# Moving four small subtractions to GpSimd and one weight sum behind another, in a two-model transformer kernel on one core

## The reference, cut to what matters

```python
def swiglu(h, w_in, w_out):                  # w_in: 1024 x 5632, w_out: 2816 x 1024
    gate, up = jnp.split(h @ w_in, 2, axis=-1)
    return (jax.nn.silu(gate) * up) @ w_out
...
x = x + FFN_HALF * swiglu(rmsnorm(x, ffn1_norm[l]), ffn1_w_in[l], ffn1_w_out[l])
x = x + hybrid_mixer(...)
x = x + FFN_HALF * swiglu(rmsnorm(x, ffn2_norm[l]), ffn2_w_in[l], ffn2_w_out[l])
```

## Time and profile before

| | |
|---|---|
| three runs | 2625.32, 2626.52, 2627.41 us; median 2626.52 |
| profiled execution | 2627.41 us, its span 2625.3 us |
| TensorE busy | 2608.7 us (99%), 15755 matmuls; granted clock 0.999 |
| VectorE busy | 2031.5 us (77%) |
| ScalarE busy | 1546.2 us (59%) |
| GpSimd busy | 116.0 us (4%) |
| DMA | 474.18 MB, mean 181 GB/s |

### The profile page before, as it was taken

One profiled execution on the slowest core, in us unless ns is written; L12 is line 12 of the kernel. 1 busy time (PEld: TensorE's weight loads), 2 busy tenths in 40 slices (PEclk: granted clock), 3 DMA queues, 4 the chain that ended last, 5 costly groups with the idle time before them and its releaser, 6 DMA issues.

```text
span 2625.3 us, 38060 instructions
## 1 busy us (share of the span) xinstructions
PE 2608.7 (99%) x15755; PEld 2293.6 (87%) x15755; DVE 2031.5 (77%) x2073; ACT 1546.2 (59%) x1703; POOL 116.0 (4%) x146
## 2 busy tenths in 40 slices
PE   9999999999999999999999999999999999999998
PEld 7889999988888899999888889999888889999887
DVE  8887854698798686547988995676997995676987
ACT  6656674465565567644656555555756555655655
POOL 0000170000000003400000000000000000000000
PEclk9999999999999999999999999999999999999999
DMA  6746545466475554545747465444755646543663
GB/s 218 241 157 200 158 145 175 136 224 227 152 239 170 170 166 160 176 130 179 245 161 232 163 206 176 153 145 153 240 193 189 204 163 193 158 137 129 225 232 104
DMA packets 388778, 474.18 MB, mean 181 GB/s; under 512 B 28855, under 2 KB 348671, under 8 KB 388352
## 3 DMA queue, kind: packets, MB, share of 16 engines
q1 hardware_dynamic: 384190, 469.86, 55.2%
q10 hardware_dynamic: 4418, 1.90, 0.3%
HBM read 466.09 MB, written 5.64 MB: 180 GB/s over the span
## 4 chain that ended last, share of the span: by engine, by line
PE 90%; DVE 5%; ACT 2%; issue 1%; DVEq 1%; DMA 0%; ACTq 0%
PE bank L421 27%; PE bank L423 27%; PE bank L422 27%; PE bank L988 1%; DVE w_lo L408 1%; PE bank L572 1%; DVE conv_acc L2165 1%; PE bank L1828 1%; PE bank L1804 1%; DVE w_lo L1216 0%; ACT w_hi L402 0%; DMA raw<-in_ffn_w_down 0%; DVEq L2977 0%; DVE part L2975 0%; DVE neg_max L2676 0%
## 5 line engine op out<-in xcount | busy, mean ns | idle before, releaser
L421 PE MATMUL bank<-w_hi,xn_hi 128*128 128x512 f32 (+2 forms) x1568 | 581.9, 371 | 1.7 <-DVE xn_lo L552 1.4
L423 PE MATMUL bank<-w_hi,xn_lo 128*128 128x512 f32 (+2 forms) x1568 | 573.1, 366 | 0.0
L422 PE MATMUL bank<-w_lo,xn_hi 128*128 128x512 f32 (+2 forms) x1568 | 572.5, 365 | 0.0
L408 DVE TENSOR_TENSOR w_lo<-raw,w_hi 128x2048 fp32r<-128x2048 f32 (+2 forms) x190 | 412.1, 2171 | 197.6 <-ACT w_hi L402 197.2
L1108 ACT ACTIVATE w_hi<-raw 128x2048 fp32r<-128x2048 f32 x192 | 367.4, 1913 | 138.2 <-DMA raw<-in_ffn_w_down 42.8
L1216 DVE TENSOR_TENSOR w_lo<-raw,w_hi 128x2048 fp32r<-128x2048 f32 x192 | 438.1, 2282 | 1.2 <-ACT w_hi L1108 1.2
L402 ACT ACTIVATE w_hi<-raw 128x2048 fp32r<-128x2048 f32 (+3 forms) x199 | 359.7, 1808 | 76.5 <-PE bank L423 74.1
L421 PE MATMUL bank<-xn_hi,w_hi 128*128 128x256 f32 (+1 forms) x1376 | 397.0, 289 | 1.0 <-DVE w_lo L408 1.0
L422 PE MATMUL bank<-xn_lo,w_hi 128*128 128x256 f32 (+1 forms) x1376 | 389.1, 283 | 0.0
L423 PE MATMUL bank<-xn_hi,w_lo 128*128 128x256 f32 (+1 forms) x1376 | 389.1, 283 | 0.0
L421 PEld LDWEIGHTS bank<-w_hi,xn_hi 128*128 128x128 f32 x1568 | 296.2, 189 | 49.7 <-DVE xn_lo L552 2.3
(11 more groups left out here) (394 smaller groups left out, 4149.7 us busy)
## 6 DMA issues: line engine op xcount, KB each, us to landing
raw<-in_w_in SPq DMA_DIRECT2D x122, 1024.0 KB, 5.3
raw<-in_ffn_w_in SPq DMA_DIRECT2D x126, 512.0 KB, 5.2
raw<-in_ffn_w_out SPq DMA_DIRECT2D x44, 1024.0 KB, 5.0
raw<-in_ffn_w_down SPq DMA_DIRECT2D x44, 1024.0 KB, 5.2
raw<-in_ffn_w_gate SPq DMA_DIRECT2D x64, 512.0 KB, 4.8
raw<-in_ffn_w_up SPq DMA_DIRECT2D x64, 512.0 KB, 6.0
block<-in_ffn_w_in SPq DMA_DIRECT2D x48, 512.0 KB, 7.1
block<-in_ffn_w_gate SPq DMA_DIRECT2D x24, 512.0 KB, 6.8
```

Source lines behind the costliest of these rows:

```text
L408: dve.tensor_tensor(in_order(kind, slot, w_lo), as_loaded(kind, slot), in_order(kind, slot, w_hi).bitcast(F32), ALU.subtract).then_inc(s_l ...
L421: pe.matmul(out, a_hi, b_hi, start=start, stop=False, skip_group_check=check)
L422: pe.matmul(out, a_hi, b_lo, start=False, stop=False, skip_group_check=check)
L423: return pe.matmul(out, a_lo, b_hi, start=False, stop=stop, skip_group_check=check)
```

## The change

1. The four `mixed_lo` subtractions of each FFN move from VectorE to GpSimd (`ffn_pool`), in the order 0, 1, 3, 2; TensorE's waits count in that order.
2. ScalarE converts the mixed tiles in other places of `first_ones`, with only number 0 ahead of the hidden values of unit 0, and both gates of unit 1 stand ahead of hi("dn", 1).
3. In the first pair of units of each FFN, VectorE runs lo("t2"), `hide`, lo("b22"), `sum_t4`, lo("t3"). The other two pairs keep the old order.
4. GpSimd's wait for the constants moves from the start of its program into `mixer1_pool`.

```diff
+        MIXED_LO = (0, 1, 3, 2)
...
+        def mixed_lo_count(f, i):
+            return 4 * f + MIXED_LO.index(i) + 1
...
             def x_mixed(i):
-                pe.wait_ge(s_xsumlo, mixed_count(f, i))
+                pe.wait_ge(s_xsumlo, mixed_lo_count(f, i))
...
             def first_ones():                      # ScalarE
                 hi("dn", 0)
-                for i in MIXED:
-                    mixed_hi(i)
+                mixed_hi(0)
                 hi_hidden(0)
+                mixed_hi(2)
                 hi("b11", 2)
-                first_gate(1)
+                gates(1)
                 hi("dn", 1)
-                second_gate(1)
+                mixed_hi(1)
                 hi_hidden(1)
+                mixed_hi(3)
                 hi("b21", 2)
                 hi("t1", 2)
...
                 lo("dn", 0)                        # VectorE, first_ones
-                mixed_lo(0)
                 lo_hidden(0)
                 sum_t1(2)
                 lo("b11", 2)
                 hide_from_bank(1, 0)
-                mixed_lo(2)
                 hide_from_bank(1, 1)
                 lo("dn", 1)
                 lo_hidden(1)
                 sum_t2(2)
                 lo("b21", 2)
                 lo("t1", 2)
-                mixed_lo(1)
                 sum_t3(2)
...
             def two(u):                            # VectorE
                 lo("t2", u)
-                sum_t4(u)
-                hide(u, 0, bank[4][:, 256:512], gate_act[:, 0, :])
                 if u == TWOS[0]:
-                    mixed_lo(3)
-                lo("b22", u)
+                    hide(u, 0, bank[4][:, 256:512], gate_act[:, 0, :])
+                    lo("b22", u)
+                    sum_t4(u)
+                else:
+                    sum_t4(u)
+                    hide(u, 0, bank[4][:, 256:512], gate_act[:, 0, :])
+                    lo("b22", u)
                 lo("t3", u)
...
+        def ffn_pool(pool, p, f):
+            def mixed_lo(i):
+                pool.wait_ge(s_xsumhi, mixed_count(f, i))
+                pool.tensor_tensor(mix_lo[i][:, :, :], mixed[i][:, :, :], mix_hi[i][:, :, :].bitcast(F32),
+                                   ALU.subtract).then_inc(s_xsumlo, 1)
+
+            for i in MIXED_LO:
+                mixed_lo(i)
...
         def mixer1_pool(pool, l):
+            pool.wait_ge(s_rest, 16 * n_rest)
...
-            pool.wait_ge(s_rest, 16 * n_rest)
-            for l in range(LAYERS):
-                mixer1_pool(pool, l)
+            for b, l in layers:
+                for k in range(2):
+                    ffn_pool(pool, in_layer(plans[b], 3 * k, l), ffn_index(b, l, k))
+                    if k == 0 and b == 0:
+                        mixer1_pool(pool, l)
```

More of the change, by code:

```diff
@@ L1111, in gate, with gates @@
                 act.activation(dst, src, ACT.Silu, scale=rstd[:, t:t + 1]).then_inc(s_gact, 1)
-            def first_gate(u):
+            def gates(u):
                 act.wait_ge(s_gu, f * len(ONES) + ONES.index(u) + 1)
                 gate(u, 0, bank[gate_bank(u)][:, 0:256], gate_act[:, 0, :])
-            def second_gate(u):
                 act.wait_ge(s_used, p.base + (FFN_AT["g1", u] + 1 + START))
                 gate(u, 1, bank[gate_bank(u) + 1][:, 0:256], gate_act[:, 1, :])
-            def gates(u):
-                first_gate(u)
-                second_gate(u)
             def hi_hidden(u):
@@ L1272, in mix @@
                 dve.tensor_tensor(mixed[i][:, :, :], in0, in1, op).then_inc(s_xsum, 1)
[L1274 to L1277, removed]
             def first_ones():
```

## The result

The changed kernel takes 2642.35 us (median of 4 runs, 2641.55 to 2643.85); the kernel before, run beside it, 2626.64 (2625.32 to 2627.41). The ratio is 1.006, 95% interval 1.0048 to 1.0072: slower by 0.6%. The profiled execution took 2642.32 us, 14.9 more than the one before.

What follows compares the result with a forecast made beforehand. TensorE, busy 2608.7 of 2625.3 us, bounds the kernel. FFN losses 7.3 + 4.8 + 0.5 and 0.4 for the load sum to 13.0 us: 2640 us forecast, range 2633 to 2647 (forecast's own 2635 to 2644).

Steps and rivals of the forecast that it cites:

- The sum t4 that moves. This is the step that decides.: First pair of units: VectorE idles, u2 comes late, t3 starts 1.69 us late; 1.83 us lost in the fifth FFN.
- between 0 and 0.7 us for an FFN; I take 0: GpSimd's subtractions delaying VectorE's lo("b22"): 0 to 6 us in all, taken as 0 since idle time holds most.
- the upper bound: GpSimd gets in at each VectorE seam, delaying it up to 3 x 1.04 us; lo("t2") ends at about 1454.5.
- This alone costs nothing: t2 starts at 1454.49.: Fifth FFN: lo("t2") ends at about 1451.45 instead of 1451.27, before t2 starts, so no cost.
- The relief is eaten by a wait.: VectorE's lo("dn", 1) starts 0.8 us later behind ScalarE's later conversion; only one removed subtraction (0.6) precedes lo("t2").
- What is late next: Way down, fifth and seventh FFN: later loads make the wait grow by some 0.2 us each, 0.4 in all.
- A: Rival: GpSimd enters VectorE's seams, holding up lo("b22"), or its last subtraction holds t3; 2643.6 to 2648.4 us, chance 0.12.
- B: Rival: sum_t4's move is hidden by misread t3 slack or ScalarE's earlier b22 conversion; 2626.6 to 2627.8 us, chance 0.08.
- C: Rival: VectorE's relief removes the waits it causes in the FFNs and t3 is not late; 2625.0 us, chance 0.04.

Runs made afterwards that it cites:

- S alone: The kernel before with only sum_t4 moved behind lo("b22") in the first pair, mixed_lo(3) staying on VectorE behind hide: 2641.9 us, ratio 1.006.
- P: The kernel before with only the four mixed_lo subtractions moved to GpSimd, whose wait for the constants moves too: 2630.1 us, ratio 1.0014.
- A alone: The kernel before with only ScalarE's new order (gates of unit 1 ahead of hi("dn", 1), mixed_hi spread out): 2630.97 us, ratio 1.0017.
- P+A: The changed kernel with sum_t4 moved back to its old place, ahead of hide, in the first pair: 2646.0 us, ratio 1.0077.

## Why the prediction was right, and where it was not

- **Direction, size and place.** Slower by 14.9 us in the profiled execution, forecast 13.0; t3 waits for `u2` in all eight FFNs, 1.5 us at most; the first FFN gives back 0.76 ahead of t1 (0.78). These held.
- **"The sum t4 that moves. This is the step that decides."** Right for the moved sum alone: `u2` and t3 to 0.02 us, unit 4 to 0.12 (15.56 for 15.44), which over eight FFNs is 1 us. Wrong for the change as a whole: there VectorE has no idle time left, and with the sum moved back the loss grows from 15.7 to 19.6 us. The forecast came true because two causes fill the same 2 us, of which I had priced one and set the other to 0. So far the hit was luck.
- **GpSimd, "between 0 and 0.7 us for an FFN; I take 0".** This is the term that failed, and the reason for the former point. GpSimd does get in at the seams: three times, as the upper bound supposed, 0.5 + 1.1 + 1.1 us. lo("t2") ended 2.33 us after t1; the forecast was -0.3, the bound 2.7. lo("b22") started at 2.65 instead of 2.51. In the changed kernel it is 15.67 us to unit 4 against the forecast 15.44: 0.23 x 8 = 1.8 of the missing 1.9 us. S alone, with nothing on GpSimd, has 15.56, so that half of this was missing from the chain itself, and half comes with P and A. That the bound was written down is what kept the range good.
- **"This alone costs nothing: t2 starts at 1454.49."** A missed wait. t2 needs `hide`, not only its own low part. With S in place it stayed hidden; A alone (4.6 us) and P+A (19.6) show what it costs without.
- **"The relief is eaten by a wait."** Right: VectorE idled 1.29 us before lo("dn", 1) (0.8 counted from its old start).
- **What is late next**, 0.4 us at the way down in two FFNs: about 0.1 by the distances from unit 4's first matmul to that point in the fifth (12.20 against 12.12) and less in the seventh. Too high.
- **Rivals.** A's mechanism was real and its price too high; B and C were not seen.

What stays open: who would go first if VectorE's and GpSimd's instructions became ready at the same moment, and whether GpSimd's four could lie in places where VectorE reads PSUM without holding anything up in any FFN. One of the four does in half of the FFNs: in the second it ends at 555.21, beside `hid_lo` and idle time of VectorE, and lengthens nothing. An order that holds all of them back until such places wasn't run.

## What to carry to other kernels

Work moved off a busy engine to one that takes turns with it is not off it: before counting 0.6 us saved, look in the trace for an instruction of each running at the same time, and price the held one. When an engine stands only tenths ahead of the one that bounds, list every wait on it in that stretch, since the nearest one hides the next; and after a forecast comes true, undo the part that was held responsible, for two causes may each fill the same gap.

## What the runs showed of the hardware

- GpSimd and VectorE took turns at whole instructions. Three GpSimd subtractions of 128x512 beside a dense VectorE queue took 9.49 us, 3.2 each, where two undisturbed products of that size took 2.04. Each let one VectorE instruction of 128x2048 pass. The first then ran beside `hid_lo` in part and made the next one take 2.79 us instead of 2.28; the other two made it 3.37 to 3.38. None of the 32 took more than 3.35 us, so VectorE's queue kept none out for longer than about one instruction.
- Between two VectorE instructions that both read SBUF twice, the cost to VectorE (1.1 us) is more than the same subtraction costs it when it does the work itself (0.6 back to back).
- A GpSimd copy with one SBUF input in the same place cost VectorE 0.41 us.
- VectorE instructions with one input in PSUM (`hide`, `hid_lo`) weren't lengthened beside GpSimd: `hid_lo` at 1446.55 took 0.68 us while a GpSimd subtraction was under way.
- TensorE's granted clock fell to 0.51 for some 3.5 us behind one stall of 2.01 us (P+A, first FFN), and not behind seven stalls of 2.07 to 2.11 us in the same execution.
